# A two-block transformer kernel: modulation chunks placed by need, own banks for a feed-forward's first step, a split scatter, and rows turned in pairs

## The reference, cut to what matters

```python
for l in range(2):                                   # first block
    mod = silu(c) @ ada_w[l] + ada_b[l]              # 6 x 1024: sh_m, sc_m, g_m, sh_f, sc_f, g_f
    hn = rmsnorm(x, mix_norm_g[l]) * (1 + sc_m) + sh_m
    a, b, c_, d = split(hn @ w_in[l])                # 3016 columns, four kinds of attention
    o = concat(diff(a), latent(b), top64_sparse(c_), band(d))
    x = x + g_m * (o @ w_out[l])
    hn = rmsnorm(x, ffn_norm_g[l]) * (1 + sc_f) + sh_f
    x = x + g_f * (swiglu(hn) if l == 0 else moe(hn))  # 2816 wide; 8 experts of 3584, top 2
x = rmsnorm(x, final_norm_g)                         # second block follows
x = x + 0.5 * rmsnorm(swiglu(rmsnorm(x)), post)      # then attention, then a second swiglu
```

## Time and profile before

| | |
|---|---|
| three runs | median 2231.89 us (2230.57 to 2233.62) |
| profiled execution | 2235.91 us |
| its span, first to last instruction | 2234.2 us |
| mean granted clock of TensorE | 0.956 of full |
| busy: TensorE, VectorE, ScalarE, GpSimd | 93%, 75%, 60%, 3% |
| read from HBM | 571 MB, 256 GB/s over the span |

### The profile page before, as it was taken

How to read it: one execution, slowest core, us unless ns; L and a number is a source line. 1 busy time by engine, 2 the same in 40 slices (tenths; PEclk the granted TensorE clock), 3 DMA queues, 4 the chain that set the end, 5 groups by cost and what they waited for, 6 DMA issues and landing times.

```text
span 2234.2 us, 26381 instructions
## 1 busy us (share of the span) xinstructions
PE 2079.2 (93%) x9638; PEld 1706.6 (76%) x9638; DVE 1670.4 (75%) x2010; ACT 1333.7 (60%) x1834; POOL 56.8 (3%) x92
## 2 busy tenths in 40 slices
PE   4958899997889999999999999999979999988998
PEld 4737788885778888787888888787857887777887
DVE  6768677765658998989898989989986555345554
ACT  2335344444437878787887878787864444465443
POOL 1010000000000000000000000000000000000000
PEclk8978899998779999999999999999999999989999
DMA  9932488741149999989898999999965554404551
GB/s 376 383 120 80 190 322 321 278 170 59 57 160 357 376 347 351 354 345 364 337 373 329 373 351 352 347 350 357 369 254 184 192 186 150 155 20 151 189 188 57
DMA packets 80616, 573.68 MB, mean 257 GB/s; under 512 B 9088, under 2 KB 9728, under 8 KB 12272
## 3 DMA queue, kind: packets, MB, share of 16 engines
q1 hardware_dynamic: 70112, 508.59, 59.9%
q0 software_dynamic: 7936, 57.05, 6.6%
q10 hardware_dynamic: 2448, 6.41, 0.8%
HBM read 570.97 MB, written 1.05 MB: 256 GB/s over the span
## 4 chain that ended last, share of the span: by engine, by line
PE 83%; DVE 9%; DMA 4%; ACT 3%; issue 1%; POOL 0%; ACTq 0%; DVEq 0%; POOLq 0%
PE ps L545 24%; PE ps L547 24%; PE ps L546 24%; DMA Z<-in_ada 3%; PE ps L913 1%; PE ps L921 1%; PE ps L888 1%; PE ps L772 1%; PE ps L500 1%; PE ps L743 1%; ACT arena L1236 1%; DVE weights_low L1617 1%; PE ps L757 1%; DVE Z L1536 1%; DMA arena<-in_ada 1%
## 5 line engine op out<-in xcount | busy, mean ns | idle before, releaser
L2054 DVE TENSOR_TENSOR weights_low<-ring,weights_high 128x1024 fp32r<-128x1024 f32 x668 | 798.8, 1223 | 62.9 <-ACT weights_high L1340 49.0
L1340 ACT ACTIVATE weights_high<-ring 128x1024 fp32r<-128x1024 f32 x668 | 706.5, 1060 | 104.2 <-PE ps L547 91.4
L545 PE MATMUL ps<-weights_high,xt_high 128*128 128x512 f32 x1832 | 736.6, 402 | 21.5 <-DVE FS L1729 6.8
L547 PE MATMUL ps<-weights_high,xt_low 128*128 128x512 f32 x1832 | 719.6, 393 | 0.0
L546 PE MATMUL ps<-weights_low,xt_high 128*128 128x512 f32 x1832 | 718.7, 392 | 0.0
L1617 DVE TENSOR_TENSOR weights_low<-ring,weights_high 128x1024 fp32r<-128x1024 f32 x298 | 362.3, 1223 | 197.6 <-ACT weights_high L1065 197.2
L1065 ACT ACTIVATE weights_high<-ring 128x1024 fp32r<-128x1024 f32 x298 | 313.5, 1058 | 319.5 <-PE ps L547 292.9
L545 PEld LDWEIGHTS ps<-weights_high,xt_high 128*128 128x128 f32 x1832 | 347.2, 190 | 94.6 <-DVE FS L1729 8.1
L547 PEld LDWEIGHTS ps<-weights_high,xt_low 128*128 128x128 f32 x1832 | 346.5, 189 | 74.0
L546 PEld LDWEIGHTS ps<-weights_low,xt_high 128*128 128x128 f32 x1832 | 347.7, 190 | 69.1 <-issue 1.5
L545 PE MATMUL ps<-weights_high,hT_high 128*128 128x512 f32 x688 | 274.0, 398 | 1.2 <-DVE hT_low L2064 1.2
(11 more groups left out here) (222 smaller groups left out, 1426.3 us busy)
## 6 DMA issues: line engine op xcount, KB each, us to landing
ring<-in_stream SPq DMA_DIRECT2D x483, 1024.0 KB, 4.9
Z<-in_ada POOLq DMA_DIRECT2D x42, 1024.0 KB, 5.3
arena<-in_ada POOLq DMA_DIRECT2D x6, 1024.0 KB, 16.3
Z<-in_na POOLq DMA_DIRECT2D x1, 2048.0 KB, 8.0
Z<-in_dil POOLq DMA_DIRECT2D x1, 2048.0 KB, 13.6
band<-in_band ACTq DMA_DIRECT2D x2, 768.0 KB, 19.9
X<-in_x SPq DMA_DIRECT2D x1, 1024.0 KB, 5.3
gate_mix<-in_rows ACTq DMA_DIRECT2D x2, 512.0 KB, 7.9
```

The source lines that it names most:

```text
L545: nc.tensor.matmul(out, xh, wh, start=n, stop=False, skip_group_check=True)
L547: return nc.tensor.matmul(out, xl, wh, start=False, stop=last, skip_group_check=True)
L1340: act.activation(WH[:, slot, :], raw, ACT.Copy).then_inc(m["hi_ready"], 1)
L2054: nc.vector.tensor_tensor(WL[:, slot, :], raw, WH[:, slot, :].bitcast(F32), ALU.subtract).then_inc(m["lo_ready"], 1)
```

## The change

- **Modulation.** 10 steps instead of 14 in and behind the first projection; 20 instead of 22 in the first feed-forward, none ahead of it; 8 instead of 2 in the second projection. The gate of the first feed-forward (`mod_row(5)`, `mod_rows`) moves from the output projection to the last step of the feed-forward and `ffn_gated`. At the start `x` is loaded behind the first chunk, weight chunks 0 and 1 behind the last two early chunks, GpSimd's further loads behind the last; the constants `cols` and `unit` have a semaphore each; step 7 stands ahead of weights.
- **Columns.** `copy_xt` is split into copy and low part, and `shifted_xt` copies one tile ahead.
- **Banks.** The first step of every feed-forward sums in banks 6 and 7.
- **Scatter.** `YE` is split into a high part (ScalarE) and a low part (VectorE, `result_low`); `CT` is fp32r; four fp32r products for a row block instead of two fp32 ones.
- **End of the experts.** The flag is loaded at their start, the last `h` is turned between two down pieces, and rows are turned in pairs.

```diff
-ADA_IN_GEMM = 14
+ADA_IN_GEMM = 10
 ADA_MIX = ADA_EARLY + ADA_IN_GEMM
 ADA_FFN = ADA_MIX + 2
+ADA_LAST = ADA_FFN + 2 * (FF_STEPS - 1)
 
...
+            sp.wait_ge(ada_full[0], 16)
             sp.dma_start(X[:, :, :], d["x"].rearrange("a (b p) n -> p (a b) n", p=P)).then_inc(x_in, 16)
...
-                if n in (0, 2):
-                    sp.wait_ge(ada_ahead[2 if n == 0 else -1], 16)
+                if n < 2:
+                    sp.wait_ge(ada_ahead[n - 2], 16)
                 sp.dma_start(ring[:, n, :], stream[n]).then_inc(full[n], 16)
...
+            pool.wait_ge(ada_ahead[-1], 16)
             load_adas(ADA_EARLY, ADA_RING)
...
-            load_adas(ADA_RING + ADA_FFN, ADA_CHUNKS - ADA_RING - ADA_FFN)
+            load_adas(ADA_RING + ADA_FFN, ADA_LAST - ADA_FFN)
             rows_roots()
+            load_adas(ADA_RING + ADA_LAST, ADA_CHUNKS - ADA_RING - ADA_LAST)
...
+            def turn_both_rows(t, source):
+
+                pe.wait_ge(turnable, TURNABLE[t] + NB)
+                for kt in range(KT):
+                    for b in range(NB):
+                        m = turned(source, root_diag[:, b, :], kt, b)
+                    if kt % 2 == 1:
+                        m.then_inc(xt_ps, 1)
 
...
-                pe.wait_ge(ada_used, (24, ADA_CHUNKS)[layer])
+                pe.wait_ge(ada_used, (ADA_FFN, ADA_CHUNKS)[layer])
                 for half in range(2):
                     mod_row(2, half, half)
                 mod_columns(3, 2)
                 mod_columns(4, 2, 8, True)
-                mod_row(5, 0, 3)
+                if layer == 1:
+                    mod_row(5, 0, 3)
...
-                    up_piece(n0 + pair // 2, pair % 2, (4, 5), pair, t)
+                    up_piece(n0 + pair // 2, pair % 2, (6, 7), pair, t)
                 for s in range(FF_STEPS - 1):
                     n, k = n0 + 2 + 3 * s, h0 + 1 + s
                     for pair in range(4):
-                        if pair == 0:
+                        if pair == 0 and s > 0:
                             pe.wait_ge(h_ready, k)
                         up_piece(n + pair // 2, pair % 2, (4, 5), pair)
                         if pair == 0:
+                            if s == 0:
+                                pe.wait_ge(h_ready, k)
...
+                        if i == 0:
+                            for half in range(2):
+                                mod_row(5, half, 4 + half)
...
-                        mm = nc.tensor.matmul(ps[:, bank + half, :], CT[:, b, :], YE[:, half * 512:(half + 1) * 512],
-                                              start=True, stop=True)
+                        nc.tensor.matmul(ps[:, bank + half, :], CT[:, b, :], YEH[:, half * 512:(half + 1) * 512],
+                                         start=True, stop=False)
+                        mm = nc.tensor.matmul(ps[:, bank + half, :], CT[:, b, :], YEL[half][:, :], start=False, stop=True)
                     mm.then_inc(m["sc_ps"], 1)
 
-                def step(c, pair, t):
+                def last_h():
+                    pe.wait_ge(m["h_ready"], EXPERTS * EX_STEPS)
...
-                        step(c, pair, 0)
+                        step(c, pair, 0, last and c == 2 * EX_STEPS - 1)
                         expert_events(c, pair, last and c >= EX_STEPS)
...
+                if m["sweep"] == 0:
+                    pe.wait_ge(route_ready, 1)
+                    overflow.append(pe.value_load(flag[0:1, 0:1], min_val=0, max_val=1))
...
-                n = EXPERTS * EX_STEPS - 1
-                pe.wait_ge(m["h_ready"], n + 1)
-                turn_h(n % 2)
-                pe.wait_ge(m["hT_ready"], n + 1)
-                downs(EX_TOTAL - 1, n, 0, 0)
+                pe.wait_ge(m["hT_ready"], EXPERTS * EX_STEPS)
...
-            with pe.If(over > 0):
+            with pe.If(overflow[0] > 0):
                 experts(moe_sems[1])
-            pe.wait_ge(turnable, TURNABLE[6] + NB)
-            turn_rows(6, YB)
+            turn_both_rows(6, YB)
...
-                    act.activation(YE, ps[:, 0:2, :].rearrange("p j n -> p (j n)"), ACT.Copy).then_inc(m["ye_ready"], 1)
+                    act.activation(YEH[:, :], ps[:, 0:2, :].rearrange("p j n -> p (j n)"), ACT.Copy).then_inc(m["ye_high"], 1)
...
+            def copy_xt(t, kt):
+
+                if kt % 2 == 0:
+                    dve.wait_ge(xt_ps, 4 * t + kt // 2 + 1)
+                sh = (0 if t % 3 == 0 else 16) + kt
+                ins = nc.vector.tensor_scalar(XT[:, kt, :], ps[:, kt // 2, (kt % 2) * T:(kt % 2 + 1) * T],
+                                              xscale[:, kt:kt + 1], modc[:, sh:sh + 1], ALU.mult, ALU.add)
+                if kt % 2 == 1:
                     ins.then_inc(xt_ready if t == 5 else xt_full, 1)
-                    if t == 5:
...
+            def shifted_xt(t, chunk, third=(), late=()):
+
+                for kt in range(3):
+                    copy_xt(t, kt)
+                xt_split_lo(t, 0)
+                ahead_lo(chunk, third)
+                copy_xt(t, 3)
+                copy_xt(t, 4)
+                xt_split_lo(t, 1)
+                ahead_lo(chunk, late[0:1])
+                copy_xt(t, 5)
+                copy_xt(t, 6)
+                xt_split_lo(t, 2)
+                copy_xt(t, 7)
+                ahead_lo(chunk, late[1:2])
+                xt_split_lo(t, 3)
+
...
-                    if g == 2 and p in (SPLITS + 1, SPLITS + 3):
-                        ada_step(ADA_CHUNKS - 2 + (p - SPLITS) // 2)
+                    if g == 2 and p % 2 == 1 and ADA_LAST + (p - SPLITS) // 2 < ADA_CHUNKS:
+                        ada_step(ADA_LAST + (p - SPLITS) // 2)
                 if g == 0:
                     lambda_sums()
-                    for a in range(2 * GEMM_GROUPS[g] - SPLITS // 2, ADA_IN_GEMM):
-                        ada_step(ADA_EARLY + a)
 
...
+                def h_both(s):
+                    dve.wait_ge(silu_ready, h0 + 1 + s)
+                    at = 4 if s else 6
+                    nc.vector.tensor_tensor(hbuf[:, :, :], sgt[:, :, :], ps[:, at:at + 2, FW:2 * FW],
+                                            ALU.mult).then_inc(h_ready, 1)
...
-                if i == 0:
-                    ada_step(ADA_FFN)
-                    ada_step(ADA_FFN + 1)
...
-                ahead_lo(GEMM_CHUNK[2], (0, 1))
+                mod_rows(gate_ffn, gate_ffn, 5, (4, 5))
+                dve.wait_ge(mod_ready, 6)
+                ahead_lo(GEMM_CHUNK[2], (0,))
...
+                def result_low(number):
+                    dve.wait_ge(m["ye_high"], number)
+                    for half in range(2):
+                        ins = nc.vector.tensor_tensor(YEL[half][:, :], ps[:, half, :],
+                                                      YEH[:, half * 512:(half + 1) * 512].bitcast(F32), ALU.subtract)
+                    ins.then_inc(m["ye_ready"], 1)
+
...
+                    if j == 1 and c > 3:
+                        result_low(e)
...
+                    if b == 1:
+                        result_low(EXPERTS)
...
+            dve.wait_ge(unit_in, 16)
             for b in range(NB):
                 set_diag(asked[b], b)
-            for a in range(3, ADA_EARLY - 1):
+            for a in range(3, ADA_EARLY):
                 ada_step(a)
-            ahead_lo(GEMM_CHUNK[0], range(2))
-            ada_step(ADA_EARLY - 1)
+            ahead_lo(GEMM_CHUNK[0], (0,))
             mod_columns(0, 0, 1, 6)
             set_xscale(0, 0)
-            for j in range(4):
-                copy_xt(0, j)
-                if j == 1:
-                    ahead_lo(GEMM_CHUNK[0], (2,))
-            ahead_lo(GEMM_CHUNK[0], (3,))
+            shifted_xt(0, GEMM_CHUNK[0], (1,), (2, 3))
             projection_lo(0)
             attention(0)
             out_gated(0)
```

138 lines of the change are left out of this document (67 added, 71 removed).

## The result

The changed kernel takes 2203.51 us (median of four runs, 2199.84 to 2205.5), the kernel before on the same chip 2232.76: a ratio of 0.9881, 95% interval 0.9865 to 0.9897, 1.2% faster. The forecast was 2190.4; the result is 13.1 above it. The profiled executions say the same: 2205.5 against 2235.91, spans 2203.8 against 2234.2, 30.4 less.

The account below looks back on a forecast made before the run. TensorE was taken to bound the experts and second projection, transfers to pace the first projection. Terms summed to -41.5 us, giving 2190.4 against the median of 2231.9; range 2180 to 2206.

Parts of the forecast that it names:

- Front: Start of the kernel: reordered loads and step 8 ahead of low parts speed the first projection, -4.5 us (-1 to -6).
- Rival B: Modulation only moved: front gains nothing (+4.5), second projection's eight steps stall TensorE (+8), 2203 us; chance 0.10.
- A: Rival: VectorE becomes the experts' bound, an expert keeps its present time, 10.5 us comes back, 2201; chance 0.12.
- D: Rival: attention 0 is held by something else, a constant or GpSimd's clearing; 14 us come back, 2204; chance 0.02.
- Four steps: End of first projection: four modulation steps moved later let attention start earlier, -14 us (-11 to -15), landing cost 0.
- Own banks: Feed-forwards: first step's sums in banks 6 and 7 remove second-step stalls and half-clock matmuls, -8.8 us (-4 to -10).
- Interleaved columns: Copying one tile ahead: 0.8 ahead of the feed-forward, 2.0 ahead of the second projection, -2.8 us (-1 to -4).
- Turning in pairs: Behind the experts: columns' copies start some 3 us earlier, but products still follow all turns, -0.5 us (to -2.5).
- Split scatter with its tail: Experts' loop: four shorter products per scatter, -10.5 us (-4 to -11.4); last scatter +0.5 (0 to +1.4).
- rival C: Experts: VectorE's lateness stops TensorE, clock falls to 1.2 GHz, kernel slower, 2252 us at 7.3 lost per expert; chance 0.02.
- Gate row: Two row products leave the first output projection, -2.5 us (-1 to -3.1), and return ending the first feed-forward, +1.7.
- The flag: Experts' flag load moved: 1.0 us off ScalarE's gap, +0.9 on TensorE between gather and first product, -0.1 (+2.2 to -2.2).

Follow-up runs that it names:

- roots_first: Changed kernel with GpSimd taking the two row-norm roots ahead of its new wait for the last early modulation chunk: 2198.22 us, ratio to before 0.9857.
- roots_and_ask_later: Changed kernel with GpSimd's roots ahead of its wait and VectorE asking for them behind modulation step 4 instead of step 1: 2193.4 us, ratio 0.983.
- x_first_roots: Changed kernel with the input asked for at once as before and GpSimd's roots ahead of its wait: 2192.1 us, ratio 0.9815.
- scatter_fp32: Changed kernel with the scatter in fp32 again, two fp32 products per row block and no subtraction on VectorE: 2215.64 us, ratio 0.9935.
- four_back: Changed kernel with the four modulation steps put back behind the first projection's last low part (14 steps there, not 10): 2215.15 us, ratio 0.9937.
- low_twice: Changed kernel with VectorE's subtraction for the low part of an expert's result made twice: 2208.98 us, ratio 0.9917.
- before_wait: Kernel before with one line added, GpSimd waiting for the last early modulation chunk before its further loads: 2244.23 us, ratio 1.0067.
- rows_apart: Changed kernel with the rows behind the experts turned block by block again: 2200.42 us, ratio 0.9878.

## Why the prediction was off, point by point

**The step that failed is "Front", -4.5 with ends -1 and -6.** It priced the order by bytes ahead of the eighth chunk, and took GpSimd's wait as a matter of its further loads only. What stands behind these loads in GpSimd's program, the roots of the row norm, was not counted, though VectorE's program asks for them between modulation steps 2 and 3 and stands still until they come. Measured: +8.75 at the first copy, 9 us at the first attention operation against the old order, instead of -4.5. A gap of 13.3, about the whole miss of 13.1; the other errors nearly cancel. Two halts made it. Taking away the one for the roots gives 5.6 us at the columns (roots_first); taking away the one for the squares as well gives another 6.7 (roots_and_ask_later). The forecast did name the input's lateness, as an end (-1), but thought of one step behind the squares; it was a halt of 7.31 us. Its premise that the projection is paced by transfers fell too: the projection's end followed the front within 2 us in every run. Without both halts the order is worth -3.3 at the attention, near the -4.5. The line of the prediction that saw columns near 30 is what roots_and_ask_later and x_first_roots show (30.53, 30.10). Rival B's first half (the front gains nothing) had the right place and the wrong cause: not bytes, but two halts; its second half is refuted. By the prediction's own sign, an attention that starts after 118, the forecast was wrong. That the time, 2203.5, lies where rivals A, B and D were put (2201 to 2204) is chance: scatter_fp32 speaks against A, four_back against B and D. The signs for the other terms came as written: no stall at the second steps, a period of 123.44, no wait for low parts in the loop.

**Four steps, -14: right.** -12.2 at the scores, -16.4 at the first operation, and 11.6 us between the medians. Landing cost 0: right for the four that four_back moved (the second projection takes 69.18 us with four steps and 69.16 with eight). The 69.46 of the kernel before is no measure of it, since the interleaved columns took 1.1 off that stage.

**Own banks, -8.8: mis-sized**, measured -3.8 in three stages. I had put the whole stalls of the earlier trace rows and the half clock behind them down to the banks; 1.41 of each is theirs. The rest of the first two stalls came from VectorE's program, a modulation step and a low part in one and the bias additions in the other, and went with other parts of the change.

**Interleaved columns, -2.8: mis-sized the other way**, -5.5, of which 4.1 in the first projection, where the sum held nothing. **Turning in pairs, -0.5: mis-sized**, -2.5. The two together take in 4.7 of the 5 us that the banks lack. The errors inside the stages cancelled, which the total alone would have hidden.

**Split scatter with its tail, -10.0: right**, -11.4 in the stages. The 0.9 given back for VectorE's lateness did not fall due: the period fell by 1.71, and low_twice finds some 0.8 us of slack behind the new work where I had worked out none. No half clock shows in the loop (granted clock 1.00 over 975 us), so rival C had no start; what the Trainium skill (TensorE: Matmul & The Clock Gate, "HAM oscillation") describes does not occur in this loop.

**Gate row, -2.5 and +1.7: not tried alone**, but the traces show the second part. TensorE in the last step of the first feed-forward, changed kernel, then before:

```profile
420.23 0.60 PE L626 MATMUL ps<-unit,FS 128*128 128x128 f32 x4
420.66 1.88 PE L685 MATMUL ps<-Z,unit 128*128 128x512 f32 x4
422.61 0.40 PE L563 MATMUL ps<-weights_low,hT_high 128*128 128x512 f32 x1
```

```profile
433.42 0.60 PE L608 MATMUL ps<-unit,FS 128*128 128x128 f32 x4
434.08 0.40 PE L546 MATMUL ps<-weights_low,hT_high 128*128 128x512 f32 x1
```

2.38 us in place of 0.66 is +1.72: right. For the first part, the stretch from the gates' first products to the feed-forward's first copy is 28.53 and 26.78 us in the two kernels with the row and 24.2 to 26.2 in the eleven without: a gain, whose size the spread hides.

**The flag, -0.1: not tried alone.** In the chain behind the experts, before and here:

```profile
1645.02 0.90 issue
1646.11 1.48 issue
```

From the last addition's end to the first high part it is 2.71 us in place of 3.46, -0.75 where I took 1.0 off; the branch still stands on the path. The load at its new place costs TensorE nothing that the trace shows: first to second gather are 56.02 us apart in both kernels, where I had put +0.9.

## What to carry to other kernels

When a change puts a wait into an engine's program, list all that is behind it in that program, with who waits for each and by when, also where the wait looks like a matter of loads only: alone, in the kernel before, such a wait cost 14 us of the front. The same list is due for a load that others are put ahead of. Here the two together cost 9 us, and moving the roots and the input ahead brought 0.7% more than the change itself. Price by stages with anchors that repeat, since a median of 2200 us hides 4 us either way and lets wrong terms cancel. A stall's length is not the price of the resource it names: put the resource back alone and see what latency is left, and read in the other engine's timeline what stood ahead of the late operation.

## What the runs showed of the hardware that I had not expected

The stage of the second attention, its output projection and the routing runs the same instructions in all kernels here and takes 127 to 135 us. Stretches from its first operation to the first gather, of the kernel before and of before_wait (columns as above; the ninth number is the granted clock):

```profile
518.64:653.71 135.07, 110.28 (x530) 89.51 (x530) 90.24 (x231) 57.70 (x149) 8.30 (x12) 0.75 0.24 89
```

```profile
533.24:660.45 127.21, 101.84 (x531) 82.44 (x531) 90.24 (x231) 57.71 (x149) 8.30 (x12) 0.81 0.24 88
```

VectorE's busy time is the same to 0.01 us, TensorE's 8.4 lower, at a mean granted clock of 0.81 in place of 0.75: more of the stage at 2.4 GHz and less at 1.2. What falls together to decide it I can't say from these runs; it does not go with the edit, since changed and before have 135.08 and 135.07, and rows_apart, whose edit lies behind the stage, has 127.19. That is most of why the profiled before_wait was only 4.8 us longer in span than before, with 14.6 lost ahead of this stage.

The input, 1 MB, took 11.2 us from its issue at 7.00 to land, behind seven chunks already queued; in the kernel before, issued at 0.89 ahead of them, it took 5.3. Here a transfer's place behind others' requests, not its size, set its time. And the front's transfers ran at 411 GB/s from 27 to 35 us and 429 from 35 to 43 in the changed kernel: the 358 of the Trainium skill (DMA: Bandwidth & Descriptors, "Where 436 GB/s comes from") that the prediction weighed is again not a limit here.
